# Whole-matrix expert weight loads, and a column-tiled decay/beta projection, in a hybrid DeltaNet and MoE layer

## The reference, cut to what matters

```python
proj = xn @ p['w_in']
(q, k, v, a_logit, b_logit, dn_gate, sc_b, sc_c, sc_h, mq, g_dn, g_sc, g_mem) = split_in(proj)
beta = jax.nn.sigmoid(b_logit)
g = -jnp.exp(p['dn_A_log']) * jax.nn.softplus(a_logit + p['dn_dt_bias'])
...
gl = jnp.minimum(xblk @ w_gate[e] + b_gate[e], SWIGLU_LIMIT)
ul = jnp.clip(xblk @ w_up[e] + b_up[e], -SWIGLU_LIMIT, SWIGLU_LIMIT)
return ((ul + 1.0) * (gl * jax.nn.sigmoid(SWIGLU_ALPHA * gl))) @ w_down[e] + b_down[e]
```

## Time and profile before

| what | value |
|---|---|
| timed runs, median | 1449.31 us (1448.35 to 1452.31, 3 runs) |
| the profiled execution's own time | 1443.22 us |
| its span | 1441.4 us |
| TensorE busy | 1387.7 us, 96% of the span |
| VectorE, ScalarE busy | 404.2 us, 231.3 us |
| read from HBM | 449.88 MB, 315 GB/s over the span |

### The profile page before, as it was taken

One profiled execution on the slowest core, in us unless ns is written; L12 is line 12 of the kernel. 1 busy time (PEld: TensorE's weight loads), 2 busy tenths in 40 slices (PEclk: granted clock), 3 DMA queues, 4 the chain that ended last, 5 costly groups with the idle time before them and its releaser, 6 DMA issues.

```text
span 1441.4 us, 16501 instructions
## 1 busy us (share of the span) xinstructions
PE 1387.7 (96%) x7295; PEld 676.0 (47%) x7295; DVE 404.2 (28%) x751; ACT 231.3 (16%) x447; POOL 0.2 (0%) x4
## 2 busy tenths in 40 slices
PE   7999999989999999999999999999999999999996
PEld 4566677645554634434434344344343443434432
DVE  3465244352112431221221221212212122122123
ACT  3334231220001111111101111111011111101112
POOL 0000000000000000000000000000000000000000
PEclk9999999999999999999999999999999999999998
DMA  9343331003472499999999999999999999999994
GB/s 335 118 134 119 117 67 60 2 4 114 166 269 117 198 387 428 427 428 427 427 427 428 427 427 428 427 428 427 428 428 427 428 426 428 427 427 427 428 427 179
DMA packets 65882, 455.62 MB, mean 316 GB/s; under 512 B 13845, under 2 KB 23226, under 8 KB 41105
## 3 DMA queue, kind: packets, MB, share of 16 engines
q1 hardware_dynamic: 65808, 454.53, 76.8%
HBM read 449.88 MB, written 4.64 MB: 315 GB/s over the span
## 4 chain that ended last, share of the span: by engine, by line
PE 77%; DMA 18%; DVE 2%; ACT 2%; issue 0%; SPq 0%; DVEq 0%
PE ps L1040 34%; DMA sb_ring<-in_w_up_dram 17%; PE ps L536 8%; PE ps L718 8%; PE ps L1017 5%; PE ps L1077 4%; PE ps L512 3%; PE ps L732 3%; PE ps L934 3%; PE ps L584 1%; DMA sb_ring<-in_w_in_dram 1%; ACT sb_xg L1440 1%; DMA sb_ring<-in_w_br_dram 1%; PE ps L813 1%; PE ps L978 0%; PE ps L823 0%
## 5 line engine op out<-in xcount | busy, mean ns | idle before, releaser
L1040 PE MATMUL ps<-sb_ring,sb_xg 128*64 128x512 f32 x2048 | 456.4, 596 | 17.1 <-DMA sb_ring<-in_w_up_dram 13.1
L1040 PEld LDWEIGHTS ps<-sb_ring,sb_xg 128*64 128x64 f32 x2048 | 140.2, 137 | 286.1 <-issue 248.4
L1040 PE MATMUL ps<-sb_ring,sb_hidT 128*64 128x512 f32 x1024 | 226.0, 594 | 0.0
L1040 PEld LDWEIGHTS ps<-sb_ring,sb_hidT 128*64 128x64 f32 x1024 | 72.0, 137 | 139.9 <-issue 137.1
L1943 DVE TENSOR_TENSOR sb_hg<-ps,sb_biases 128x512 f32<-128x512 f32 x32 | 22.1, 691 | 403.7 <-PE ps L512 403.7
L718 PE MATMUL ps<-sb_xn,sb_ring 128*128 128x384 f32 x384 | 134.7, 496 | 0.0
L536 PE MATMUL ps<-sb_xn,sb_ring 128*128 128x384 f32 x384 | 127.7, 491 | 1.6 <-DMA sb_ring<-in_w_in_dram 1.6
L1967 DVE TENSOR_TENSOR sb_h<-sb_h,ps 128x512 f32<-128x512 f32 x96 | 61.5, 683 | 135.6 <-PE ps L1077 125.8
L536 PEld LDWEIGHTS ps<-sb_xn,sb_ring 128*128 128x128 f32 x384 | 72.9, 192 | 51.4 <-issue 1.9
L718 PEld LDWEIGHTS ps<-sb_xn,sb_ring 128*128 128x128 f32 x384 | 71.4, 191 | 48.9 <-issue 4.6
L1017 PEld LDWEIGHTS ps<-sb_onehot,sb_xn 128*128 128x128 f32 x720 | 81.5, 192 | 12.2 <-issue 12.2
(11 more groups left out here) (302 smaller groups left out, 955.1 us busy)
## 6 DMA issues: line engine op xcount, KB each, us to landing
sb_ring<-in_w_gate_dram SPq DMA_DIRECT2D x64, 2048.0 KB, 32.0
sb_ring<-in_w_up_dram SPq DMA_DIRECT2D x64, 2048.0 KB, 30.9
sb_ring<-in_w_down_dram SPq DMA_DIRECT2D x64, 2048.0 KB, 28.9
sb_ring<-in_w_in_dram SPq DMA_DIRECT2D x12, 2048.0 KB, 9.8
sb_ring<-in_w_br_dram SPq DMA_DIRECT2D x2, 2048.0 KB, 8.2
sb_ring<-in_w_o_dram SPq DMA_DIRECT2D x2, 2048.0 KB, 16.8
sb_ring<-in_w_mem_kv_dram SPq DMA_DIRECT2D x1, 2048.0 KB, 15.4
sb_ring<-in_cache_mem_k_dram SPq DMA_DIRECT2D x1, 2048.0 KB, 13.8
```

The costliest lines, as they stand in the source:

```text
L1040: last = mm(o, x(k), columns(kind, w, i, j), start=(k == 0), stop=(k == KT8 - 1))
```

## The change

Three things. Matrices 12 to 93 (82 of the 96) are loaded by one request of 4 MB into two slots that lie side by side, with one semaphore for both halves; the first twelve and the last two stay halves. For this the slots' order becomes (2, 3), (0, 1), (4, 5) and the two of `ring2`, and the first pieces wait for other trunk pieces. Decay and beta are made from eight matmuls with `wab` (now 32 columns wide, of which eight count) as stationary operand and all 384 tokens as moving one, in four column tiles of 32, each tile summing two of the eight row blocks; ScalarE copies the 128 x 384 result, and three small matmuls with a constant 128 x 8 matrix (`fold`) add the four tiles and turn the result. And the pieces change places: memory tile 0 is piece 12, decay and beta 13, memory tile 1 piece 14, with banks of their own.

```diff
-        wab = lay("wab", [P, KT8, 8])
+        wab = lay("wab", [P, KT8, 32])
-        PJ_WAB, PJ_MEM, PJ_MQ, PJ_SC, PJ_GATE, PJ = 12, 13, 15, 17, 23, 27
+        PJ_MEM, PJ_WAB, PJ_MQ, PJ_SC, PJ_GATE, PJ = (12, 14), 13, 15, 17, 23, 27
+        ab4 = wk[:, 1024:1024 + TOK]
         def pj_bank(q):
+            if NQKV <= q < PJ_SC:
+                return (1, 2, 0, 3, 1)[q - NQKV]
             return q % 4 if q < PJ_SC else 1 + q % 3
...
-        SLOTS = (3, 1, 2, 0, 4, 5, 6, 7)
+        def pair(q):
+            k = q // 2 % 4
+            return ring2 if k == 3 else ring[:, (2, 0, 4)[k]:(2, 0, 4)[k] + 2, :]
         def slot(q):
+            return pair(q)[:, q % 2, :]
+        def is_whole(q):
+            return 12 <= q // 2 < 3 * E - 2
+        def signals(q):
+            return not (is_whole(q) and q % 2)
...
+            def whole(kind, expert, q):
+                src = weights[kind][expert:expert + 1, :, :, :]
+                dma(pair(q).rearrange("p a (t n) -> p (a t) n", t=4), src.rearrange("e p t n -> p (e t) n"))\
+                    .then_inc(piece_in[q % 8], 16)
...
             sp_.wait_ge(S["out"], 64)
+            through(13)
             half("gate", 0, 0, 0)
+            half("gate", 0, 1, 1)
             through(12)
-            half("gate", 0, 1, 1)
-            through(13)
+            through(14)
             half("up", 0, 0, 2)
-            through(14)
             half("up", 0, 1, 3)
...
-                for k in range(2):
-                    q = order(kind, n) + k
-                    sp_.wait_ge(S["used"], q - 7)
-                    half(kind, n, k, q)
+                q = order(kind, n)
+                if is_whole(q):
+                    sp_.wait_ge(S["used"], q - 6)
+                    whole(kind, n, q)
+                else:
+                    for k in range(2):
+                        sp_.wait_ge(S["used"], q + k - 7)
+                        half(kind, n, k, q + k)
...
-            pe.wait_ge(S["wab_in"], 16)
-            bank_free(PJ_WAB)
-            for a in range(TILES):
-                for t in range(KT8):
-                    last = mm(bank(pj_bank(PJ_WAB))[:, a * 8:(a + 1) * 8], xnT[:, t, a * P:(a + 1) * P], wab[:, t, :],
+            pe.wait_ge(S["vec_in"], 80)
+            pe.wait_ge(S["pjev"], 9)
+            for k in range(2):
+                for r in range(4):
+                    last = mm(bank(0)[32 * r:32 * r + 32, 0:TOK], wab[:, 4 * k + r, :], xnT[:, 4 * k + r, :], start=(k == 0), stop=(k == 1))
+            last.then_inc(S["abp"], 1)
             pe.wait_ge(S["xT"], 5)
             weights_in(3)
-            for a in range(2):
...
+            memory_columns(0)
+            bank_free(PJ_WAB)
+            pe.wait_ge(S["abc"], 1)
+            for a in range(TILES):
+                last = mm(bank(pj_bank(PJ_WAB))[:, a * 8:(a + 1) * 8], ab4[:, a * P:(a + 1) * P], const("fold"), start=True, stop=True)
+            last.then_inc(S["pj"], 1)
+            memory_columns(1)
...
+                    if landed(q) is not None:
+                        pe.wait_ge(piece_in[q % 8], landed(q))
...
+            act.wait_ge(S["abp"], 1)
+            f(ab4, bank(0)[:, 0:TOK], ACT.Copy).then_inc(S["abc"], 1)
+            evacuate(PJ_MEM[0])
             evacuate(PJ_WAB)
```

More of the change, by code:

```diff
@@ L26 @@
     ("before", P), *((f"level{s}", 64) for s in LEVELS), ("upto64_prompt", 64), ("upto64_sample", 64), ("ident64", 64),
-    ("seq4", 4), ("slots2", 2 * CAP), ("rounds", 24),
+    ("seq4", 4), ("slots2", 2 * CAP), ("rounds", 24), ("fold", 8),
 ):
@@ L58, in constant_table @@
     put("rounds", np.arange(24)[None, :])
+    put("fold", i % 32 == np.arange(8)[None, :])
     return table
@@ L291, in build @@
         PIECES = 6 * E
+        LANDED = [16 * sum(signals(p) for p in range(q % 8, q + 1, 8)) for q in range(PIECES)]
+        LANDED_ALL = [16 * sum(signals(p) for p in range(s, PIECES, 8)) for s in range(8)]
         BIAS_ROUND = {8: 0, 9: 1, 10: 2}
@@ L391, in _ @@
             dma(hb[:, 4:8], A["dn_dt_bias"].partition_broadcast(P).rearrange("p o h -> p (o h)")).then_inc(S["vec_in"], 16)
-            dma(wab[:, :, :], win[:, :, 1536:1544]).then_inc(S["wab_in"], 16)
+            dma(wab[:, :, :], win[:, :, 1536:1568]).then_inc(S["vec_in"], 16)
             for n in (2, 3, 4, 5, 6):
@@ L545, in norm_sums @@
                 last.then_inc(S["nsum"], 1)
-            pe.wait_ge(S["cst"], 16)
+            pe.wait_ge(S["cst"], 32)
             for t in range(TILES):
@@ L569, in _, with memory_columns @@
             tokens_turned(4)
-            pe.wait_ge(S["wab_in"], 16)
-            bank_free(PJ_WAB)
-            for a in range(TILES):
+            def memory_columns(a):
+                q = PJ_MEM[a]
+                bank_free(q)
                 for t in range(KT8):
-                    last = mm(bank(pj_bank(PJ_WAB))[:, a * 8:(a + 1) * 8], xnT[:, t, a * P:(a + 1) * P], wab[:, t, :],
+                    last = mm(bank(pj_bank(q)), mT[:, t, a * P:(a + 1) * P], piece(TRUNK_SLOT[3])[:, t, :],
                               start=(t == 0), stop=(t == KT8 - 1))
-            last.then_inc(S["pj"], 1)
+                last.then_inc(S["pj"], 1)
[5 more added lines that the diff above has]
+            last.then_inc(S["abp"], 1)
             pe.wait_ge(S["xT"], 5)
             weights_in(3)
-            for a in range(2):
-                bank_free(PJ_MEM + a)
-                for t in range(KT8):
-                    last = mm(bank(pj_bank(PJ_MEM + a)), mT[:, t, a * P:(a + 1) * P], piece(TRUNK_SLOT[3])[:, t, :],
-                              start=(t == 0), stop=(t == KT8 - 1))
-                last.then_inc(S["pj"], 1)
+            memory_columns(0)
[3 more added lines that the diff above has]
+                last = mm(bank(pj_bank(PJ_WAB))[:, a * 8:(a + 1) * 8], ab4[:, a * P:(a + 1) * P], const("fold"), start=True, stop=True)
+            last.then_inc(S["pj"], 1)
+            memory_columns(1)
             norm_sums(1)
@@ L1031, in product @@
                     q = q0 + piece_
-                    pe.wait_ge(piece_in[q % 8], landed(q))
+                    if landed(q) is not None:
+                        pe.wait_ge(piece_in[q % 8], landed(q))
                     w = slot(q).rearrange("p (t n) -> p t n", t=4)
@@ L1043, in landed @@
             def landed(q):
-                return 16 * (q // 8 + 1)
+                return LANDED[q] if signals(q) else None
             def gathered(i):
@@ L1150, in again @@
                         def again(q):
-                            return 16 * i + 16 * (PIECES // 8) + 16
+                            return 16 * i + LANDED_ALL[q] + 16
                         pe.wait_ge(S["accrd"], 6 * r)
@@ L1208, in evacuate @@
                     last = f(xp_sample(q), b[:, 256:TOK].rearrange("p (s k) -> p s k", k=LS), ACT.Copy)
-                elif q < PJ_MEM:
+                elif q == PJ_WAB:
                     last = f(small[:, 64:88], b[:, 0:24], ACT.Copy)
                 elif q < PJ_MQ:
-                    last = f(kvp[:, q - PJ_MEM, :], b, ACT.Copy)
+                    last = f(kvp[:, PJ_MEM.index(q), :], b, ACT.Copy)
                 elif q < PJ_SC:
@@ L1263, in _ @@
             f(small[:, 144:156], small[:, 88:100], ACT.Sigmoid).then_inc(S["abg"], 1)
-            evacuate(PJ_MEM)
-            evacuate(PJ_MEM + 1)
+            evacuate(PJ_MEM[1])
             norm_root(1)
@@ L1559, in _ @@
             x_scaled(2)
-            dve.wait_ge(S["n1_in"], 16)
+            dve.wait_ge(S["cst"], 32)
             for t in range(TILES):
@@ L1615, in _ @@
             conv(9)
-            dve.wait_ge(S["vec_in"], 64)
+            dve.wait_ge(S["vec_in"], 80)
             x_weighted(3)
@@ L1627, in _ @@
             az = small[:, 192:204].rearrange("p (a k) -> p a k", a=3)
-            dve.wait_ge(S["pjev"], PJ_MEM)
+            dve.wait_ge(S["pjev"], PJ_WAB + 1)
             link(v.tensor_tensor(az, lgt[:, :, 0:4], hb[:, 4:8].unsqueeze(1).to_broadcast([P, 3, 4]), ALU.add))
```

10 lines of the change are left out of this document (4 added, 6 removed).

## The result

The changed kernel takes **1439.82 us** (median of 4 runs, 1438.7 to 1440.49) against 1449.31 us; the ratio is 0.9929, with a 95% interval of 0.9905 to 0.9954. The forecast, 1447.4 us, was too high, and its range, 1442 to 1453 us, misses the time at the lower end. A fourth timed run of the kernel before took 2416.5 us; it is left out of its median, and no trace shows why it was so long.

The account below looks back on a forecast made before the run. The end was taken as a moment in the expert-weight DMA stream plus TensorE's remaining work. Stream -4.3, end +2.2 and decay and beta +0.2 us gave -1.9 us: 1447.4 us, range 1442 to 1453.

Parts of the forecast that it names:

- I carry differences over unchanged: Whole kernel: the difference worked out for the profiled execution, 1443.22 us, was applied as it stood to the median, 1449.31.
- Term 1: Expert weight stream: fewer, longer packets save 6 ns each, 54 ns a matrix, so up(30) lands 4.3 us earlier (2.0 to 5.3).
- What a request costs beside its bytes: Expert weight stream: this cost of each DMA request was taken as hidden behind the requests ahead of it.
- Term 2: End of the kernel: TensorE begins up(30) only when all of it has landed, costing 2.2 us (to 3.4).
- The later issue: DMA issue: SP waits until both slots are free; taken as 0 us, bound 2.4 us once.
- Term 3: Decay, beta and memory projection: 0.5 us won at its start, 0.7 lost by the fold; +0.2 us (-1.7 to +0.6).
- The lag: Rival, weight stream: engines' falling behind is halved for pieces made whole, 3.4 us more gained, 1444.0 us; chance 0.22.
- Packets did not stay at 16 KB: Rival, weight stream: 4 MB still moves as 16 KB packets, saving only 0.5 us, 1451.2 us; chance 0.13.
- 32 KB packets weren't slower: Rival, weight stream: a 32 KB packet takes 4 ns more than two of 16 KB, 1454.3 us; chance 0.08.
- the 0.3% that carried the largest chance: Whole kernel: a median within 0.3% of the kernel before, 1445.0 to 1453.7 us, was given chance 0.60.
- faster by over 0.3%: Whole kernel: a median under 1445.0 us, from most of the lag rival and the forecast's edge where the clock stays up; 0.28.

Follow-up runs that it names:

- experiment 1: The changed kernel unchanged, timed again beside fresh runs of the kernel before: 1444.70 us, ratio 0.9967.
- experiment 7: Changed kernel with one request per whole matrix, but three of every four in 16 KB packets; against the kernel before: 1451.89 us, ratio 1.0022.
- experiment 9: Changed kernel with each whole matrix sent as two requests, each over every second partition, in 32 KB packets; against the kernel before: 1445.93 us, ratio 0.9954.
- Experiment 12: Changed kernel with little added filling matmuls, and whole matrices from the fifth instead of the thirteenth; against the kernel before: 1442.30 us, ratio 0.9946.
- experiment 4: Changed kernel with up(30), gate(31) and down(30) back in halves; against the kernel before: 1446.91 us, ratio 0.9964.
- experiment 11: Changed kernel with a few unread matmuls in TensorE's idle stretches before the memory projection and around the router's last tile; against the kernel before: 1437.63 us, ratio 0.9896.
- experiment 10: The changed kernel unchanged, timed a third time beside the kernel before: 1442.37 us, ratio 0.9948.

## Why the prediction was right or wrong

- **Range and time: wrong.** The step that failed first is "I carry differences over unchanged" from one profiled execution to the medians. The forecast difference was -1.9 us, the profiles' -4.6, the medians' -9.5. The last isn't the change's: run again, it gave 0.9967 and 0.9948, and at one clock -3.7 and -3.8 us. The range held the unknown costs of the edit, and nothing for the clock that a handful of runs happens to get, though the extremes of 35 runs of the kernel before lie 14 us apart. The four runs stood at a mean clock of 0.991, those of experiment 1 at 0.9878; at 1.37 us for each 0.001 that is 4.4 of the 4.9 us between their medians, by this estimate. Why those four runs had it higher isn't known.
- **Term 1, the stream: mechanism right, size too small.** Forecast 54 ns a matrix (25 to 66), 4.3 us. Measured 73 ns: about 71 for eight packets of 32 KB instead of sixteen of 16 KB, 9 ns for each packet less, where the term took 6 and its upper bound 7.3. The lines drawn on from packets of 2 KB and 4 KB through those of 16 KB gave too small a fixed part for the next doubling; why, stays open. The landings came closer together than the forecast's 6 ns for each packet explains. All in all the stream lost 5.5 us between these two profiles and 6.1 by the means of the ten.
- **What a request costs beside its bytes, taken as hidden: right.** Experiments 7 and 9 bear out: one request or two differ by some 3 ns a matrix at most.
- **Term 2, the end: right.** 35.67 us forecast, 35.7 measured, +2.2.
- **The later issue at no cost: right** where it was made. From the end of the first product to the first whole matrix's landing it is 88.8 us, 88.9 before. Experiment 12 shows the price where the queue is empty, 3.4 us.
- **Term 3, decay and beta: right in sum** (+0.2 forecast, -0.1 +- 0.6 measured) and in its parts. Eight matmuls took 1.50 us (1.4), the fold 0.73 (0.7). The memory projection starts at VectorE's release, at 88.85 us and not 87.9, because this profile's trunk stood 1.06 us later; counted from the start of decay and beta, 0.6 us are won, where 0.5 were forecast. The sum holds no gain from the clock: its fall is there in six of the eight profiles with this projection and no filling. Its lower bound uses 1.7 us, which no run shows as it stands; it is an estimate from the earlier trace rows, 3.65 us x (1.00 - 0.53). In the profile after, where the clock stayed at 1.00, the two memory tiles took 7.13 and 7.11 us, 14.2 together, against 15.68 before: 1.4 us.
- **Two slips in the working** change little: Term 3's lower bound is 0.2 - 1.7 = -1.5 us, not -1.7, and three matrices at the forecast 9.84 us take 29.5 us, not 29.2.
- **The rivals.** The lag did not go: 8.3 us between the engines at the end, 8.1 before. Packets did not stay at 16 KB; experiment 7 shows what that would have been, 1.0022. 32 KB packets weren't slower.
- **The chances.** At one clock the change is worth -3.7 us of 1446, 0.26%: inside the 0.3% that carried the largest chance, nearly at its edge. The first measurement fell into "faster by over 0.3%", for which 0.28 stood; but that was built on the lag, which did not go, and on the clock of one short stretch, while by the estimate above the clock over the whole launch brought it there. That was luck of the draw, and speaks neither for nor against the rivals.

## What to carry to other kernels

Where a DMA stream sets the end, as here, look for longer contiguous runs before fewer requests: the former gave 6.1 us of stream here, the latter nothing that shows (experiments 7 and 9). Size the gain from landings of many equal pieces, since a few nanoseconds in a packet decide it: 11 of 1226 here. Leave the first pieces small while the queue is shallow; whole matrices from the fifth on lengthened the stream by 3.4 us in experiment 12. Whether it pays to leave the last ones small, where the consumer begins before the whole has landed, experiment 4 did not show. Before a difference of 0.5% is put down to an edit, compare the mean granted clock of the runs (0.001 of it went with 1.37 us here); and look at what stands idle ahead of a stretch at the lower level, because filling it was worth as much here as the change: 4.7 us in experiment 11, where the change gives 3.7.

## What was not expected of the hardware

- Requests for partitions 0 to 63 and 64 to 127 ran at 211 GB/s, those for every second partition at 430: 2504 and 1214 ns for a packet of 32 KB.
- Going from packets of 16 KB to 32 KB saved some 9 ns for each packet less; the small packet that tells of the end took 9 ns by its record and some 3 ns at most of the spacing.
- Spans follow the mean granted clock at 1.3 to 1.4 us per 0.001; the extremes of 35 runs of one kernel lie 14 us apart.
- Less than 4 us of added matmuls around the router's last tile took away a stretch at a clock of 0.50, 10.2 us long in experiment 10.
